# Routing logits from the residual stream, the norm beside them, and the first expert's rows by one-hot products

## The chip, the cores and the metric

One Trainium2 chip, one of its cores. The engines are TensorE (PE, with its weight loads PEld), VectorE (DVE), ScalarE (ACT), GpSimd (POOL) and SyncE (SP), which here only issues transfers. The metric is the device time of one execution in microseconds (us), the median of several runs.

## The reference

A hybrid decoder layer: an RWKV-7 branch and a block-sparse attention branch are merged and projected, the result is added to the input, and a hierarchical mixture of experts follows. The change lies between the output projection and the first expert. What is computed there, for 512 tokens of width 1024:

```python
x = x + gate1 * jnp.einsum('bsd,de->bse', merged, w_out[l])
h2 = rms_norm(x, ln2_g[l]) * (1.0 + scale2) + shift2
x = x + gate2 * hierarchical_moe(h2, w_rg[l], b_rg[l], w_re[l], b_re[l], w1[l], w3[l], w2[l])

# in hierarchical_moe
p_group = jax.nn.softmax((ht @ w_rg + b_rg).astype(f32), axis=-1)      # 4 groups, the best one is taken
e_logits = (ht @ w_re + b_re).astype(f32).reshape(T, N_GROUPS, EXPERTS_PER_GROUP)
# in the group taken: softmax over 8 experts, the two best, their weights made to sum to pg_top
hid = jax.nn.silu(lax.ragged_dot(xs, w1, sizes)) * lax.ragged_dot(xs, w3, sizes)
ys = lax.ragged_dot(hid, w2, sizes) * weights...                        # 32 experts, width 512
```

## The kernel before

All data is float32. A token tile is 128 tokens, so there are TT = 4 tiles, and KT = 8 blocks of 128 channels. The order of each engine's work is written out by hand; engines wait on semaphores by name and count (`x2_done`, `h2_v`, `out_mm` and so on), and every wait holds up all that stands behind it on its engine.

The output projection is 8 groups of 24 matmuls on PE: four token tiles for the left half of the channels, then four for the right half. `out_mm` counts them. DVE adds each group to the residual stream x (`residual`, two instructions of 512 columns), counted by `x2_done`. ACT squares and sums each half row (`half_square`). When both halves of a tile are there, DVE does `norm2(t)`: sum, the root by ACT, the reciprocal, and for each half h2 = x * r * a2, then h2 + shift2. a2 is the gain (1 + scale2) * ln2_g.

PE then turns h2 (`turn_h2`, 8 transposes for a tile, into banks 2 and 3), ACT copies the turned tile to `h2T` and stores the plain one to the table `h2_table` in memory (`turned_h2`), and PE multiplies `h2T` with the routing weights `w_route` (36 columns: 4 groups and 32 experts) in `logits(t)`, 8 matmuls. Only tile 0 is turned ahead of the last projection group.

DVE adds the bias and picks: group, then expert one and two, each by maximum and comparison. The picks go to PE, which counts each token's rank within its expert (four matmuls). From rank and pick DVE makes `slot_hot`, and PE the slot table (`fill_table`): which token sits in which of the 64 slots of an expert, and with what weight. From it DVE makes `slot_rows`, and POOL gathers 64 rows of `h2_table` for each expert by an indirect DMA (`gather`), two experts ahead. PE turns these rows (`do_rows`), ACT copies them to `xT`, and then `up` (w1 and w3 side by side, 16 instructions each), `turn_hid` and `down` follow for each of 32 experts.

The expert weights are three matrices of 2 MB each, in a ring of three slots (`W1_IN`, `W3_IN`, `W2_IN`). SyncE issues them in the order w1, w3, w2 for each expert. A slot's w1 and w3 are free after `up` of three experts ago (`up_mm`), its w2 after `down` (`w2_mm`). The first loads have other gates, since their slots lie in buffers of the earlier phases: w2 of expert 0 waits for the fourth projection group, everything of expert 1 and w1 of expert 2 for the eighth (`out_mm` 8), w3 of expert 2 (its buffer holds h2) for the stores of h2 and all turns, w2 of expert 2 (its buffer holds `h2T`) for the logits. The tenth load, w1 of expert 3, waits for `up` of expert 0.

## Time and profile before

| | us |
|---|---|
| median of 3 runs | 1155.04 (1154.87 to 1158.41) |
| profiled execution, its own time | 1153.15 |
| its span, first to last instruction | 1151.2 |
| eighth projection group ends | 603.0 |
| picks ready | 622.1 |
| first row gather issued | 630.1 |
| expert 0's up-projection | 641.7 to 651.3 |
| last instruction | 1151.2 |

PE is busy 86% of the span, DVE 40%, ACT 27% and POOL 16%; the mean granted clock of TensorE is 0.943 of its full speed. The page cuts the span into 40 slices of 28.8 us. The busy share of the DMA engines is 9 or more (tenths) in the slices from about 660 us to 1120 us, and the last half of the span is spent on the 32 experts. Times of stretches are read as start and end within the span; "idle before" is the engine's idle time just before an instruction, and the arrow names what ended it.

### The profile page before, as it was taken

Reading aid. Unit: us, or ns where it says so; the run is one execution under the profiler, and the core shown is the slowest. Engines: PE = TensorE matmul, PEld = TensorE weight load, DVE = VectorE, ACT = ScalarE, POOL = GpSimd, SP = SyncE. Lnnn points to the kernel's source line nnn. Section 1 sums busy time; section 2 is a strip of 40 time slices with the busy share of each in tenths; the row PEclk is TensorE's granted clock in tenths of the full one; section 3 lists DMA queues with packets and bytes.
Section 4 is the critical chain, followed back from the end, with each engine's and each line's share of the span. In section 5 each row is a group of like instructions: output and inputs, shape, how many; then the busy total and the mean of one; then the engine's idle time right before and its main releaser. Section 6 shows DMA issues by size and latency. Waiting matters only on the chain.

```text
span 1151.2 us, 18827 instructions
## 1 busy us (share of the span) xinstructions
PE 988.6 (86%) x8256; PEld 646.5 (56%) x8256; DVE 462.4 (40%) x724; ACT 315.7 (27%) x537; POOL 182.5 (16%) x201
## 2 busy tenths in 40 slices
PE   3799999898988889999994799998788787978786
PEld 3567799798985668788784333333333333333332
DVE  4548861635427856676565221111111111111115
ACT  6367752042326861222322111110111011100110
POOL 0000000460994430000000011111011110111101
PEclk9799999898979999999997799999899999999998
DMA  9331121400003047465729699999999999999995
GB/s 365 142 147 55 72 76 38 149 15 3 5 3 147 8 165 256 146 224 179 291 100 389 245 407 408 404 392 405 402 406 409 414 407 401 412 410 416 409 398 204
DMA packets 52578, 285.64 MB, mean 248 GB/s; under 512 B 8970, under 2 KB 13210, under 8 KB 38672
## 3 DMA queue, kind: packets, MB, share of 16 engines
q1 hardware_dynamic: 46432, 272.81, 60.5%
q0 software_dynamic: 5056, 8.31, 2.2%
q10 hardware_dynamic: 1008, 3.31, 0.7%
q8 instruction: 66, 1.08, 0.4%
q14 instruction: 16, 0.13, 0.0%
HBM read 276.19 MB, written 16.25 MB: 254 GB/s over the span
## 4 chain that ended last, share of the span: by engine, by line
PE 58%; DMA 28%; DVE 8%; ACT 3%; issue 2%; SPq 1%; DVEq 0%; ACTq 0%; POOLq 0%
PE banks L1566 26%; DMA w_ring<-in_w 21%; PE banks L2001 11%; PE banks L2015 4%; DMA w_tok<-in_w 4%; DMA zr<-in_w_ada 2%; PE banks L1717 1%; PE banks L1719 1%; PE banks L1732 1%; DMA picked<-h_table,slot_rows 1%; PE banks L1859 1%; DVE tokm_r L1032 1%; DVE ring L1170 1%; PE banks L1607 1%; PE banks L1753 1%
## 5 line engine op out<-in xcount | busy, mean ns | idle before, releaser
L2001 PE MATMUL banks<-w_ring,xT 128*64 128x512 f32 x336 | 151.3, 604 | 30.7 <-DMA w_qkv<-in_w 16.4
L850 ACT ACTIVATE silu_a<-banks 64x512 f32<-64x512 f32 x32 | 18.9, 591 | 408.8 <-PE banks L2002 408.8
L1492 DVE TENSOR_TENSOR hid<-banks,silu_a 64x512 f32<-64x512 f32 x32 | 22.2, 693 | 258.6 <-ACT silu_a L850 258.6
L2001 PEld LDWEIGHTS banks<-w_ring,xT 128*64 128x64 f32 x336 | 45.6, 139 | 128.1 <-issue 128.1
L1480 DVE SCALAR_TENSOR_TENSOR mod<-banks,row_weight,mod 64x512 f32<-64x512 f32 x64 | 47.8, 748 | 164.3 <-PE banks L2015 163.3
L2015 PE MATMUL banks<-w_ring,hidT 128*64 128x512 f32 x352 | 92.1, 671 | 10.4 <-ACT hidT L854 10.4
L2001 PE MATMUL banks<-w_ab,xT 128*64 128x512 f32 x176 | 84.9, 639 | 16.8 <-DMA w_tok<-in_w 16.2
L940 POOL DMA_INDIRECT y_rows<-mod,slot_rows x30 | 27.7, 923 | 402.6 <-DVE mod L1480 387.2
L2002 PE MATMUL banks<-w_tok,xT 128*64 128x512 f32 x176 | 85.1, 640 | 0.0
L2002 PE MATMUL banks<-w_ring,xT 128*64 128x512 f32 x176 | 77.7, 594 | 0.0
L1566 PE MATMUL banks<-x_r,ring_r 128*128 128x512 f32 x192 | 77.1, 401 | 0.6 <-DVE tokm_r L1032 0.6
L2002 PE MATMUL banks<-w_qkv,xT 128*64 128x512 f32 x160 | 73.9, 617 | 0.0
L1566 PE MATMUL banks<-ring_r,hT_r 128*128 128x256 f32 (+1 forms) x224 | 69.3, 332 | 2.0 <-DVE zr_r L1032 2.0
L2001 PEld LDWEIGHTS banks<-w_ab,xT 128*64 128x64 f32 x176 | 25.1, 147 | 71.5 <-issue 70.6
L2015 PEld LDWEIGHTS banks<-w_ring,hidT 128*64 128x64 f32 x352 | 26.0, 153 | 60.1 <-issue 46.7
L1292 DVE SCALAR_TENSOR_TENSOR mod<-ada_buf,small,mod 128x512 f32<-128x512 f32 x64 | 48.0, 750 | 11.1 <-DMA ada_buf<-in_w_ada 6.2
L1994 PEld LDWEIGHTS banks<-consts,picked 64*128 64x128 f32 x256 | 30.6, 200 | 35.8 <-issue 24.3
L1566 PE MATMUL banks<-x_r,tokm_r 128*128 128x512 f32 x128 | 49.8, 389 | 0.0
L701 ACT ACTIVATE ring<-banks 128x512 f32<-128x512 f32 (+1 forms) x64 | 33.1, 517 | 59.4 <-PE banks L1732 27.4
L1566 PE MATMUL banks<-ring_r,x_r 128*128 128x256 f32 x256 | 47.8, 288 | 0.2 <-DVE ring_r L1032 0.2
L1566 PEld LDWEIGHTS banks<-ring_r,hT_r 128*128 128x128 f32 x224 | 42.8, 191 | 6.6 <-issue 2.8
L1994 PE MATMUL banks<-consts,picked 64*128 64x64 f32 x256 | 35.1, 278 | 11.2 <-DMA picked<-h_table,slot_rows 11.2
(367 smaller groups left out, 2182.4 us busy)
## 6 DMA issues: line engine op xcount, KB each, us to landing
w_ring<-in_w SPq DMA_DIRECT2D x54, 2048.0 KB, 36.7
w_tok<-in_w SPq DMA_DIRECT2D x21, 2048.0 KB, 38.9
w_ab<-in_w SPq DMA_DIRECT2D x11, 2048.0 KB, 34.8
w_qkv<-in_w SPq DMA_DIRECT2D x10, 2048.0 KB, 39.4
ada_buf<-in_w_ada SPq DMA_DIRECT2D x64, 256.0 KB, 3.2
tokm<-in_w_gate SPq DMA_DIRECT2D x3, 2048.0 KB, 13.5
ring<-in_w_mix SPq DMA_DIRECT2D x5, 1024.0 KB, 4.8
ring<-in_w_ada SPq DMA_DIRECT2D x2, 2048.0 KB, 14.3
```

The lines of the kernel that those rows point to most:

```text
L701: act.activation(dst.rearrange("p h n -> p (h n)"), src, ACT.Copy).then_inc(solve_a[k], 1)
L850: act.activation(silu_a[:, :], bank[2][0:SLOTS, :], ACT.Silu).then_inc(silu_done, 1)
L940: pool.indirect_dma_start(y_rows, IOA(slot_rows[:, 1, e:e + 1].bitcast(u32), 0), ys[:, e % 2, :], None, bounds_check=2 * SEQ - 1, oob_is_e ...
L1032: dve.tensor_tensor(dst, src, hi_.bitcast(f32), ALU.subtract).then_inc(cut_v, 1)
L1292: dve.scalar_tensor_tensor(mod[:, n, :], ada_buf[:, q % NADA, :], small[:, 8 + k:9 + k], mod[:, n, :], ALU.mult, ALU.add).then_inc(ada_use ...
L1480: dve.scalar_tensor_tensor(dst[:, 512 * n:512 * n + 512], bank[5 + n][SLOTS * n:SLOTS * n + SLOTS, :], weight_of(e), gate2[:, n, :], ALU.m ...
L1492: dve.tensor_tensor(hid[:, :], bank[3][SLOTS:P, :], silu_a[:, :], ALU.mult).then_inc(hid_v, 1)
L1566: mm = pe.matmul(dst, a[i][:, k, col_a], b[l][:, k, col_b], start=(k == 0 and n == 0), stop=(k == nk - 1 and n == 2))
L1994: mm = pe.transpose(turned(b)[:, k, :], picked[0:SLOTS, b, k:D:KT], ident[0:SLOTS, 0:SLOTS])
L2001: pe.matmul(bank[2][0:SLOTS, :], xT[:, b, k, :], w1[:, k, :], start=(k == 0), stop=(k == KT - 1))
L2002: mm = pe.matmul(bank[3][SLOTS:P, :], xT[:, b, k, :], w3[:, k, :], start=(k == 0), stop=(k == KT - 1))
L2015: mm = pe.matmul(bank[5 + n][SLOTS * n:SLOTS * n + SLOTS, :], hidT[:, k, :], w2[:, k, 512 * n:512 * n + 512], start=(k == 0), stop=(k == 3))
```

## The change

- The norm's scale r is one number for a token, so it can be taken out of the product with the routing weights: logits = r * (x @ (gain * w_route)) + (shift2 @ w_route + bias). PE turns x instead of h2 (`turn_x2`, one half tile at a time, in the order `x2_turns`), as soon as `residual` has made it, between the projection groups. The logits of a tile have a bank of their own, and DVE scales them by r and adds the bias (`logits_of`).
- For that the gain and the shift are turned into columns (`norm_columns`, 16 transposes of one row), the routing weights are multiplied by the gain column on DVE, and PE computes shift2 @ w_route (`route_bias`, 8 matmuls).
- `norm2` is now one half tile at a time and stands between the residuals; the half (3, 1) comes after the picks. The stores of h2 are a step of their own on ACT (`store_h2`), the last one behind both exponentials.
- After the logits PE does 20 matmuls of the identity with itself, whose result is not used (`keep_running_to_picks`).
- Expert 0's rows are not gathered. DVE makes `first_hot` (token by slot, for expert 0) from the first column of the ranks, and PE computes the turned rows as h2 times `first_hot` (`first_rows`, 8 blocks of 4 matmuls, 64 columns each), half of them ahead of the slot table and half behind it. POOL gathers from expert 1 on.
- w2 of expert 2 is issued before w3 of expert 2; the latter waits for the stores and for `first_rows`, which read h2 there.
- The sum and reciprocal of the group's exponentials move behind the picks. Several semaphores are merged (`s_late`, `ov_in`).

The core of the diff:

```diff
             def load_w13(e):
...
                 if e == 2:
+                    load_w2(2)
                     sp.wait_ge(h2_stored, 16 * TT)
-                    sp.wait_ge(h2t_mm, KT)
+                    sp.wait_ge(xt_mm, 1)
                 sp.dma_start(W3_IN[c], w3_src[e]).then_inc(w3_in[c], 16)
...
+            turned_x2(0)
+            turned_x2(1)
+            spread(0)
+            turned_x2(2)
+            turned_x2(3)
+            turned_x2(4)
+            spread(1)
+            store_h2(0)
+            turned_x2(5)
+            spread(2)
+            turned_x2(6)
+            spread(3)
+            turned_x2(7)
+            store_h2(1)
+            store_h2(2)
+            for i in range(1, 3):
                 act.wait_ge(exp_in, i)
                 ap = gtmp if i == 1 else stats[5]
                 act.activation(ap, ap, ACT.Exp).then_inc(exp_out, 1)
+            store_h2(3)
...
-            gather(0)
             gather(1)
+            gather(2)
...
+            def logits_of(t):
+                dve.wait_ge(logit_mm, t + 1)
+                return dve.scalar_tensor_tensor(L[:, t, :], bank[LOGIT_BANK[t]][:, 0:NR], ln_stat[:, 12 + t:13 + t], b_route, ALU.mult, ALU.add)
...
+            residual(TT)
+            norm2_scale(0)
+            dve.wait_ge(cols_mm, 1)
+            dve.tensor_copy(rt[:, 1000:1016], bank[1][:, 496:512]).then_inc(cols_v, 1)
+            norm2(0, 0)
+            norm2(0, 1)
+            residual(TT + 1)
+            dve.wait_ge(cols_mm, 2)
+            seq(dve.tensor_tensor(b_route, b_route, bank[1][:, 0:NR], ALU.add))
+            dve.tensor_tensor(w_route, w_route, gain_col.unsqueeze(2).to_broadcast([P, KT, NR]), ALU.mult).then_inc(cols_v, 1)
...
+            residual(TT + 3)
+            norm2_scale(3)
+            for t in range(TT - 1):
+                logits_of(t)
+            norm2(3, 0)
+            seq(logits_of(3))
...
+            norm2(3, 1)
+            ranks_of_first = bank[1][:, 0:TT * NEXP].rearrange("p (t n) -> p t n", n=NEXP)[:, :, 0]
+            dve.wait_ge(rank_mm, 1)
+            seq(dve.tensor_copy(first_rank, ranks_of_first))
+            for t in range(TT):
+                ins = dve.tensor_scalar(first_hot[:, t, :], const("slot_id"), first_rank[:, t:t + 1], PICKS[:, t, 0:1], ALU.is_equal, ALU.mult)
+            ins.then_inc(cols_v, 1)
...
                     mm = three_passes(bank[4 + j % TT][:, :], (m_hi, m_lo), cut_views(i), k,
                                       slice(P * (j % TT), P * (j % TT) + P), slice(0, 512))
+                    if j == 2 * TT - 1 and k == 4:
+                        turn_x2(6)
                 mm.then_inc(out_mm, 1)
-                if j == 2 * TT - 2:
-                    turn_h2(0)
...
+                if j == TT:
+                    turn_x2(0)
+                    turn_x2(1)
+                    norm_columns()
+                elif j == TT + 1:
+                    turn_x2(2)
+                    turn_x2(3)
+                    turn_x2(4)
+                    pe.wait_ge(s_late, 96)
+                    route_bias()
+                elif j == TT + 2:
+                    turn_x2(5)
+                    logits(0)
+
             logits(1)
             logits(2)
-            turn_h2(3)
-            logits(3).then_inc(logit_mm, 1)
+            turn_x2(7)
+            logits(3)
+            keep_running_to_picks(20)
             pe.wait_ge(picks_v, 1)
...
+            def first_rows(ks):
+
+                for k in ks:
+                    for t in range(TT):
+                        mm = pe.matmul(turned(0)[:, k, :], h2[:, t, k:D:KT], first_hot[:, t, :], start=(t == 0), stop=(t == TT - 1))
+                return mm
+
+            pe.wait_ge(h2_v, 2 * TT)
+            pe.wait_ge(cols_v, FIRST_HOT)
+            first_rows(range(0, 4))
             pe.wait_ge(slots_v, 1)
...
-            do_rows(0)
+            first_rows(range(4, KT)).then_inc(xt_mm, 1)
```

How the instructions stand now, at three places.

PE between the seventh and the eighth projection group (the 128x512 rows are the projection; 36 columns are logits). Before:

```order
L1566 MATMUL banks<-ring_r,hT_r 128x512 x2
L1566 MATMUL banks<-ring_r,zr_r 128x512
L1566 MATMUL banks<-ring_r,hT_r 128x512 x2
L1566 MATMUL banks<-ring_r,zr_r 128x512
L1938 MATMUL banks<-consts,w_qkv 128x128 [waits h2_v]
L1938 MATMUL banks<-consts,w_qkv 128x128 x3
L1938 MATMUL banks<-consts,w_qkv 128x128 [waits h2_v]
L1938 MATMUL banks<-consts,w_qkv 128x128 x3
L1566 MATMUL banks<-ring_r,hT_r 128x512 [waits x2_done]
L1566 MATMUL banks<-ring_r,hT_r 128x512
L1566 MATMUL banks<-ring_r,zr_r 128x512
```

Now, at the same place:

```order
L1615 MATMUL banks<-ring_r,zr_r 128x512
L1615 MATMUL banks<-ring_r,hT_r 128x512 x2
L1615 MATMUL banks<-ring_r,zr_r 128x512
L1987 MATMUL banks<-consts,x 128x128 [waits h2t_a,x2_done]
L1987 MATMUL banks<-consts,x 128x128 x3
L2014 MATMUL banks<-consts,w_tok 128x36 [waits cols_v,h2t_a]
L2014 MATMUL banks<-consts,w_tok 128x36 x7
L1615 MATMUL banks<-ring_r,hT_r 128x512 [waits x2_done]
```

One turn of h2 (8 transposes) has become half a turn of x (4 transposes) and the logits of tile 0. Ahead of the fifth, sixth and seventh group stand the other new pieces, and the turn numbered 6 stands within the eighth.

PE from the picks to the first expert. The rows of 32 and 96 columns right behind the wait for `picks_v` are the ranks, 64x96 is the slot table, and `w_ab` holds w1 of expert 0. Before:

```order
L1976 MATMUL banks<-mod,consts 128x32 [waits picks_v]
L1977 MATMUL banks<-mod,consts 128x96
L1978 MATMUL banks<-mod 128x96
L1979 MATMUL banks<-mod 128x32
L1985 MATMUL banks<-consts,mod 64x96 [waits slots_v]
L1985 MATMUL banks<-consts,mod 64x96 x7
L1994 MATMUL banks<-consts,picked 128x64 [waits rows_in0]
L1994 MATMUL banks<-consts,picked 128x64 x7
L2001 MATMUL banks<-w_ab,xT 64x512 [waits w3_in0,w1_in0,xt_a]
L2002 MATMUL banks<-w_tok,xT 64x512
```

Now:

```order
L2014 MATMUL banks<-consts,w_tok 128x36 [waits h2t_a]
L2014 MATMUL banks<-consts,w_tok 128x36 x7
L2007 MATMUL banks<-consts 128x128 x20
L2055 MATMUL banks<-mod,consts 128x32 [waits picks_v]
L2056 MATMUL banks<-mod,consts 128x96
L2057 MATMUL banks<-mod 128x96
L2058 MATMUL banks<-mod 128x32
L2071 MATMUL banks<-consts,w_qkv 128x64 [waits cols_v,h2_v]
L2071 MATMUL banks<-consts,w_qkv 128x64 x15
L2064 MATMUL banks<-consts,mod 64x96 [waits slots_v]
L2064 MATMUL banks<-consts,mod 64x96 x7
L2071 MATMUL banks<-consts,w_qkv 128x64 x16
```

The wait for gathered rows (`rows_in0`) and the 8 transposes are gone; 32 products of h2 (in `w_qkv`) take their place, on both sides of the slot table, with a wait for `first_hot` and the last half of h2.

SyncE from the fourth load of the ring (w1 of expert 1) to the twelfth. Before, the fifth row here (`w_qkv`) is w3 of expert 2 and the sixth (`w_tok`) its w2; now the fifth is w2 and the sixth w3. Before:

```order
L455 DMA w_ring<-in_w 128x4096 [waits out_mm]
L459 DMA w_ring<-in_w 128x4096
L469 DMA w_ring<-in_w 128x4096
L455 DMA w_ring<-in_w 128x4096
L459 DMA w_qkv<-in_w 128x4096 [waits h2t_mm,h2_stored]
L469 DMA w_tok<-in_w 128x4096 [waits logit_mm]
L455 DMA w_ab<-in_w 128x4096 [waits up_mm]
L459 DMA w_tok<-in_w 128x4096
L469 DMA w_ring<-in_w 128x4096 [waits w2_mm]
```

Now:

```order
L461 DMA w_ring<-in_w 128x4096 [waits out_mm]
L466 DMA w_ring<-in_w 128x4096
L476 DMA w_ring<-in_w 128x4096
L461 DMA w_ring<-in_w 128x4096
L476 DMA w_tok<-in_w 128x4096 [waits logit_mm]
L466 DMA w_qkv<-in_w 128x4096 [waits xt_mm,h2_stored]
L461 DMA w_ab<-in_w 128x4096 [waits up_mm]
L466 DMA w_tok<-in_w 128x4096
L476 DMA w_ring<-in_w 128x4096 [waits w2_mm]
```

The last two loads of the first nine have changed places, and w3 of expert 2 waits for the turned rows of expert 0 instead of the last turn of h2.

## Rows read from the trace of the kernel before

**Rows 1.** windows: us, busy (x) of each engine, PEclk, DMA share, GB/s.
```profile
604.00:628.00 24.00, 13.14 (x101) 12.51 (x101) 13.49 (x49) 5.87 (x12) 0.00 (x0) 0.75 1.01 413
628.00:629.00 1.00, 0.68 (x5) 0.38 (x3) 0.25 (x2) 0.00 (x0) 0.00 (x0) 0.50 0.14 49
629.00:642.00 13.00, 1.49 (x10) 1.25 (x12) 7.94 (x41) 0.98 (x2) 2.25 (x3) 0.50 0.97 341
642.00:652.00 10.00, 10.00 (x48) 3.47 (x44) 0.00 (x0) 1.49 (x2) 0.72 (x1) 0.76 0.07 18
652.00:1100.00 448.00, 379.54 (x1751) 152.50 (x1750) 66.30 (x95) 45.45 (x87) 53.70 (x58) 0.95 1.01 406
```

**Rows 2.** chain of waits from 700 us: start us, us, what.
```profile
774.93 41.21 DMA w_tok<-in_w
```

**Rows 3.** timeline, SyncE: start us, us, queue, line, issue, out<-in.
```profile
603.04 0.33 SPq L455 DMA_DIRECT2D w_ring<-in_w  x1
...
604.37 0.51 SPq L455 DMA_DIRECT2D w_ring<-in_w  x1
...
628.52 1.30 SPq L469 DMA_DIRECT2D w_tok<-in_w  x1
651.32 0.33 SPq L455 DMA_DIRECT2D w_ab<-in_w  x1
```

**Rows 4.** chain of waits, 550 to 660 us: start us, us, what.
```profile
630.09 9.69 DMA picked<-h_table,slot_rows
...
641.00 0.61 ACT xT L845
...
641.65 1.12 PE banks L2001
```

**Rows 5.** timeline, PE: start us, us, line, instruction, out<-in, shapes, count [idle before].
```profile
596.48 1.04 PE L1938 MATMUL banks<-consts,w_qkv 128*128 128x128 f32 x8
...
607.32 3.66 PE L1945 MATMUL banks<-consts,w_tok 128*128 128x36 f32 x32
...
612.13 1.97 PE L1945 MATMUL banks<-consts,w_tok 128*128 128x36 f32 x16 [0.25 <-ACT w_tok L821]
622.16 0.64 PE L1976 MATMUL banks<-mod,consts 128*128 128x32 f32 x2 [8.05 <-DVE mod L1395]
...
625.86 2.82 PE L1985 MATMUL banks<-consts,mod 128*64 128x96 f32 x16 [1.78 <-DVE mod L1423]
```

**Rows 6.** timeline, DVE, the same columns.
```profile
607.37 0.74 DVE L1345 SCALAR_TENSOR_TENSOR w_qkv<-x,consts,mod 128x512 f32<-128x512 f32 x1
...
614.22 0.31 DVE L1372 TENSOR_TENSOR consts<-banks,consts 128x144 f32<-128x144 f32 x1 [5.38 <-PE banks L1945]
...
615.60 0.18 DVE L1376 TENSOR_TENSOR consts<-consts 128x16 f32<-128x16 f32 x1
...
616.47 0.17 DVE L1381 TENSOR_SCALAR consts<-consts 128x16 f32<-128x16 f32 x1
...
621.46 0.64 DVE L1395 TENSOR_TENSOR mod<-mod 128x32 f32<-128x32 f32 x3
...
625.11 0.69 DVE L1423 TENSOR_TENSOR mod<-consts 128x512 f32<-128x512 f32 x1
```

**Rows 7.** timeline, PE, 22 to 27 us, while the clock falls.
```profile
22.64 0.36 PE L1546 MATMUL banks<-small,tokm 128*128 128x1 f32 x2
22.87 0.36 PE L1547 MATMUL banks<-small,tokm 128*128 128x1 f32 x2
...
26.20 0.56 PE L1547 MATMUL banks<-small,tokm 128*128 128x1 f32 x2
26.62 0.56 PE L1546 MATMUL banks<-small,tokm 128*128 128x1 f32 x2
```

**Rows 8.** DMA issues of 611 to 613 us: x, KB, us to landing.
```profile
h_table<-w_qkv ACTq DMA_DIRECT2D x1, 512.0 KB, 16.2
```

**Rows 9.** windows, columns as in rows 1: 332 to 343 us.
```profile
332.00:343.00 11.00, 10.26 (x177) 10.10 (x177) 1.53 (x3) 1.28 (x5) 10.39 (x10) 0.53 0.01 1
```

More of the change, by code:

```diff
@@ L475, in _ @@
                 load_w13(e)
-                load_w2(e)
+                if e != 2:
+                    load_w2(e)
             for b in range(2):
@@ L1336, in residual, with norm2_scale @@
                 dve.tensor_tensor(xx, xx, out_sc[:, j % 4, :], ALU.add).then_inc(x2_done, 1)
-            def norm2(t):
+            def norm2_scale(t):
                 dve.wait_ge(ssq2, TT + 2 * t + 1)
@@ new lines, in norm_columns, with route_bias @@
+            def norm_columns():
+                pe.wait_ge(cols_v, GAIN2)
+                for i, row in enumerate((mod[0:1, 4:6, :], mod[0:1, 2:4, :])):
+                    row = row.rearrange("p a n -> p (a n)")
+                    for k in range(KT):
+                        at = 496 + KT * i + k
+                        mm = pe.transpose(bank[1][:, at:at + 1], row[:, P * k:P * k + P], ident[0:1, 0:1])
+                mm.then_inc(cols_mm, 1)
+            def route_bias():
+                pe.wait_ge(cols_v, COLUMNS)
+                for k in range(KT):
+                    mm = pe.matmul(bank[1][:, 0:NR], shift_col[:, k:k + 1].to_broadcast([P, P]), w_route[:, k, :], start=(k == 0), stop=(k == KT - 1))
+                mm.then_inc(cols_mm, 1)
@@ L1941, in logits, with keep_running_to_picks @@
+            def keep_running_to_picks(n):
+                for _ in range(n):
+                    pe.matmul(bank[2][:, 0:P], ident, ident, start=True, stop=True)
             def logits(t):
+                pe.wait_ge(h2t_a, TT + t + 1)
+                if t == 0:
+                    pe.wait_ge(cols_v, ROUTE_W)
                 for k in range(KT):
-                    if k % 4 == 0:
-                        pe.wait_ge(h2t_a, 2 * t + k // 4 + 1)
-                    mm = pe.matmul(bank[0][:, NR * t:NR * t + NR], h2T[:, k, P * t:P * t + P], w_route[:, k, :], start=(k == 0), stop=(k == KT - 1))
@@ L1946, in logits @@
-                return mm
+                    mm = pe.matmul(bank[LOGIT_BANK[t]][:, 0:NR], h2T[:, k, P * t:P * t + P], w_route[:, k, :], start=(k == 0), stop=(k == KT - 1))
+                mm.then_inc(logit_mm, 1)
             for j in range(2 * TT):
```

118 lines of the change are left out of this document (58 added, 60 removed).

## The prediction

> **What bounds the kernel now.** I read the windows first, then SyncE's timeline, the chain of waits, and the timelines of PE and DVE around the norm and the routing. From 652 us on the kernel is a stream of expert weights: the DMA share is 1.01 at 406 GB/s until 1100 us [rows 1], and in the chain a load is on the path with 41.21 us from issue to landing [rows 2]. Every us after 652 is therefore bytes over bandwidth, and the change does not touch those bytes. What can be won lies before. The ring of three slots takes nine loads (experts 0 to 2). Seven of them are issued by 604.37, with a wait on the last out-projection matmul at 603.04; the last two come at 628.15 and 628.52, after the h2 rows are stored and the logits are done; the tenth is issued at 651.32, when expert 0's up-projection has ended [rows 3]. The DMA engines are full from 604 to 628 (413 GB/s), nearly idle for 1 us, busy again from 629 to 642, and then idle for ten: 18 GB/s between 642 and 652 [rows 1]. That hole is what the change aims at. Expert 0 is late because its rows are fetched from memory: the gather takes 9.69 us, the copy of the turned rows ends at 641.6 and the up-projection starts at 641.65 [rows 4].
>
> So the end of the kernel follows the later of two times. One is E, when expert 0's up-projection ends and frees its slot. The other is D, when the first nine loads, the stores and two gathers are through. Before, E = 651.3 and D = 641.5. Nothing flows before 652, so from the issue at 651.32 to the first bytes I count 1.1 us: the stream restarts at 652.4.
>
> **The change, step by step.**
>
> PE before the last out-projection ends. Every out-projection group is 5.44 us. Before, one turn of h2 (8 transposes) stands between groups 7 and 8; it costs 0.88 us of the 1.04 shown, 0.11 each [rows 5]. Now there stand in front of the end of group 8: seven turns of x (28 transposes, 3.1 us); 16 one-column turns of gain and shift; 8 bias matmuls; 8 matmuls of logits(0). The logits of a tile are 16 instructions, two for each matmul; 32 take 3.66 us, so 16 take 1.76 in a row [rows 5], and I give the bias and logits(0) 1.76 each. No row shows a one-column turn of one partition. The nearest are the transposes at 0.11: 1.76 us, with 0.6 as the lower end if a load of one row is cheap. The fifth turn reuses a bank whose copy by ACT takes 0.6 us [rows 4]: 0.5 of stall. Sum: 3.1 - 0.9 + 1.8 + 1.8 + 1.8 + 0.5 = 8.0 us, 6.5 to 9. The eighth group ends at 611.0 instead of 603.0, and so do the four loads that wait for it start 8 us later. This is the price of the change.
>
> D. Before, the same bytes went through in 36.0 us: from 604.3 (1.2 after the issues) to 641.5, less the hole of about 1.2 us. In the new order the w2 load of expert 2 waits only for the logits (issued near 618), and its w3 load waits for the end of the one-hot products (637 or later). The five loads and three stores ahead of it keep the engines busy until 612.3 + 29.2 = 641.5 (12.06 MB at 413 GB/s). So the hole at 628 is gone, unless the products end after 640. D = 612.3 + 36.0 = 648.3, between 646.8 and 649.3.
>
> Logits. logits(1) and (2) end at 614.6. The last turn, its copy and logits(3) follow: 0.44 (four transposes of 0.11), 0.85 (a copy of 0.6 with the hand-overs) and 1.96 [rows 4, 5], thus 617.9, where before it was 614.1. The scaled logits stand at 618.1. DVE's pieces of the norm (0.75 and 0.69 us each, [rows 6]) lie beside these matmuls; only norm2(3, 0) is near, from 615.2 to 616.7, and is hidden.
>
> Picks. Before, 614.56 to 622.1, with an exponential waited for, a sum and a reciprocal in between (615.8 to 616.5) [rows 6]. Without these 0.7 us the chain is 6.9: picks at 625.1, 3.0 later than before.
>
> One-hot rows. DVE does norm2(3, 1) (1.44) while PE ranks the picks (1.9 us, [rows 5]); the copy of the ranks and four 64-column compares at about 0.2 follow: 628.0. The weights and slots then take 3.75 us instead of 3.35: 631.8. PE does 32 matmuls of 64 columns, 64 instructions, half of them before the slot table and half after. Their price hangs on TensorE's clock, and here the trace speaks clearly: with 128 stationary columns and one moving column two instructions start 0.23 us apart at the full level and 0.42 apart after the clock had fallen to 1.2 GHz [rows 7], 0.11 and 0.21 each. So 7.1 us or 13.6 us. Moving 64 columns fits under the weight load at both levels. The slot table costs 1.4 or the 2.8 of the row, which ran at 0.50.
>
> The Trainium skill ("TensorE: Matmul & The Clock Gate", LDWEIGHTS) gives a weight load as its columns over 1.2 GHz, 107 ns whatever the level. By that the products would be an estimated 6.8 us at either level (64 times 107 ns), and the slow rival C below would fall away. The rows speak against it, and they decide.
>
> E. Warm throughout: 628.0 + 3.5, slot table from 631.8 to 633.2, + 3.6 = 636.8; copy 0.65; up-projection 6.85 (it is 9.6 in the trace, with five us at half clock): E = 644.3. With the clock low for the first five us: 646.8. Both are before D less the 1.1 us, 647.2, so in both cases D decides.
>
> Beside this. Store 3 now leaves at 626.9 instead of 611.9. A store took 16.2 us beside full queues [rows 8], but that was the third in a row; behind one that lands at 628 or so, I expect 635. The gathers of experts 1 and 2 then land near 646, and PE meets them at E + 0.9: at most 1 us of stall after E, in a stretch where DMA is ahead. One gather fewer is 0.26 MB in the old hole, worth nothing. The merged semaphores and the overflow loop cost nothing here. The queue behind the waiting w3 load on SyncE holds only loads that wait for E anyway.
>
> **Sum.** The stream restarts at 648.3 instead of 652.4: 4.1 us less. Against its own 1153.15 (span 1151.2) the profiled execution would be 1149.0. That execution lies 1.9 below the median of 1155.04; on the median I get 1150.9, with 1149 to 1152 for this case.
>
> **Rivals.**
>
> A, the forecast: E is early enough and D decides, 1150.9.
>
> B, the clock stays low for part of the products. PE idles from the end of the 20 filler matmuls (40 instructions at 0.11 from 617.9: 622.3) to the picks, and again for some 1.5 us until first_hot. Before, it fell to 0.50 after the logits and was still there at the slot table [rows 1, 5]. If it rises near 640, E is 649 to 651 and the gain is 0 to 2.3: 1154.
>
> C, slower: the clock does not rise before the up-projection. What speaks for it is the stretch from 332 to 343 us, where PE was 93% busy with small matmuls and had 0.53 of its clock [rows 9]. Products and table would be 6.8 + 2.8 + 7.0 from 628.0, 644.6, copy to 645.3, up-projection at the old 9.6: E = 654.9, 3.6 later than 651.3: 1158.6. It turns from gain to loss when products and table together exceed 13 us, with the up-projection then cold as before. Against it: the products keep PE without a gap for over 7 us, and the filler shortens the idle time from 8 us to under 3.
>
> D', the change does not do what it says: out-projections are held up by more than counted (a turn that waits for DVE's residual, since DVE now does the norm between residuals). With 12 us instead of 8 the gain is gone: 1155. Each residual has over 2 us of slack in my timetable, so this is unlikely.
>
> **Chances.** A 0.53, B 0.18, C 0.22, D' 0.07. A measurement of this kernel tells 0.3%, 3.5 us, from no change. A lies just beyond it: of its 0.53 I give 0.40 to faster and 0.13 to the same; B and D' are the same; C splits, 0.17 slower and 0.05 the same; 0.02 of B goes to faster. Faster 0.42, same 0.41, slower 0.17. The range leaves out the tails of A and C: 1148.5 to 1159.0.
>
> **What would show it.** Right: the last out-projection ends near 611; DMA without a hole from 612 to the end; up-projection of expert 0 ends before 647; the tenth load is issued then. B or C: PEclk of 0.5 between 628 and 645 and products at 0.21 us per instruction. Wrong altogether if the stream after the restart has another length than the 470 us of before, or if the out-projection ends elsewhere than 609.5 to 612.

## The result, and the profile after

The changed kernel takes 1160.13 us (median of 20 runs), the kernel before 1154.7 us beside it: a ratio of 1.0042, with an interval of 1.0027 to 1.0057. By the ratio that is 4.8 us slower (by the two medians 5.4) where 4.1 us faster was forecast, and 1.1 us above the top of the range that I gave. The profiled execution has a span of 1157.0 us, where the one before had 1151.2.

The windows after, with the columns of [rows 1] (us, busy time of PE, PEld, DVE, ACT, POOL, then the granted clock of TensorE, DMA share, GB/s):

```profile
612.00:628.00 16.00, 13.24 (x86) 12.70 (x85) 11.09 (x46) 3.24 (x7) 0.00 (x0) 0.79 0.97 404
628.00:642.00 14.00, 13.91 (x62) 13.60 (x63) 6.25 (x23) 0.00 (x0) 1.54 (x2) 0.63 0.92 387
642.00:652.00 10.00, 9.31 (x31) 5.84 (x33) 5.26 (x31) 1.88 (x2) 0.51 (x1) 0.54 0.53 184
652.00:662.00 10.00, 9.52 (x60) 4.63 (x58) 1.30 (x5) 1.46 (x3) 0.00 (x0) 0.94 0.51 180
```

The hole that the change aims at has not gone. It lay at 642 to 652 and now lies at about 641 to 657, and one load fills less than half of it. SyncE's timeline (start, duration, queue, line, issue) shows why, beside [rows 3]:

```profile
580.08 0.33 SPq L476 DMA_DIRECT2D w_ring<-in_w  x1
610.46 0.33 SPq L461 DMA_DIRECT2D w_ring<-in_w  x1
618.33 0.33 SPq L476 DMA_DIRECT2D w_tok<-in_w  x1
646.63 0.33 SPq L466 DMA_DIRECT2D w_qkv<-in_w  x1
657.27 0.33 SPq L461 DMA_DIRECT2D w_ab<-in_w  x1
```

The load at 610.46 waits for the eighth projection group: 7.4 us later than before. The load of w3 of expert 2 waits for the end of the one-hot products and leaves at 646.63. The tenth load waits for expert 0's up-projection and leaves at 657.27 instead of 651.32. PE's timeline says where that time is (beside [rows 5]):

```profile
618.11 6.75 PE L2007 MATMUL banks<-consts 128*128 128x128 f32 x40
628.09 7.90 PE L2071 MATMUL banks<-consts,w_qkv 128*128 128x64 f32 x32 [1.57 <-DVE consts L1447]
635.92 2.82 PE L2064 MATMUL banks<-consts,mod 128*64 128x96 f32 x16
638.67 7.88 PE L2071 MATMUL banks<-consts,w_qkv 128*128 128x64 f32 x32
647.24 1.11 PE L2090 MATMUL banks<-w_ab,xT 128*64 128x512 f32 x1 [0.69 <-ACT xT L870]
```

The one-hot products (L2071) take 7.9 us for each half, 15.7 us in all, with the slot table's 2.75 between them. The up-projection starts at 647.24 at half clock and ends at 657.2.

### The profile page after: what moved, and what is told of

It reads as the page before. It is cut to its first block, busy times and chain, and to the rows that moved or that the text cites. A ratio compares the mean times of both kernels' runs of the same rounds, so it can differ in the third digit from the quotient of the medians.

```text
span 1157.0 us, 19096 instructions
## 1 busy us (share of the span) xinstructions
PE 1017.1 (88%) x8384; PEld 672.5 (58%) x8384; DVE 464.8 (40%) x735; ACT 316.0 (27%) x537; POOL 181.6 (16%) x200
## 4 chain that ended last, share of the span: by engine, by line
PE 59%; DMA 27%; DVE 8%; ACT 3%; issue 2%; SPq 1%; DVEq 0%; ACTq 0%
PE banks L1615 26%; DMA w_ring<-in_w 21%; PE banks L2090 11%; PE banks L2104 4%; DMA w_tok<-in_w 4%; DMA zr<-in_w_ada 2%; PE banks L1766 2%; PE banks L2071 1%; PE banks L1768 1%; PE banks L1781 1%; PE banks L1908 1%; PE banks L2014 1%; DVE tokm_r L1057 1%; DVE ring L1195 1%; PE banks L1656 1%
## 5 line engine op out<-in xcount | busy, mean ns | idle before, releaser
L2104 PE MATMUL banks<-w_ring,hidT 128*64 128x512 f32 x352 | 93.6, 680 | 10.4 <-ACT hidT L879 10.4
L1615 PEld LDWEIGHTS banks<-x_r,ring_r 128*128 128x128 f32 x192 | 37.5, 195 | 9.1 <-DVE tokm_r L1057 1.0
## 6 DMA issues: line engine op xcount, KB each, us to landing
w_ring<-in_w SPq DMA_DIRECT2D x54, 2048.0 KB, 36.2
```

Of the source, the lines that this page charges most:

```text
L1615: mm = pe.matmul(dst, a[i][:, k, col_a], b[l][:, k, col_b], start=(k == 0 and n == 0), stop=(k == nk - 1 and n == 2))
L2104: mm = pe.matmul(bank[5 + n][SLOTS * n:SLOTS * n + SLOTS, :], hidT[:, k, :], w2[:, k, 512 * n:512 * n + 512], start=(k == 0), stop=(k == 3))
```

## A ruler for the runs

Profiled executions differ by up to 8 us before anything of interest here starts: the fourth projection group ends between 578.9 and 586.4. So I read each trace from that point, which SyncE marks by its load of w2 of expert 0 (580.08 in the rows above). Three stretches remain: from there to the end of the eighth group (called g8 from here on, read at the first load that waits for it), from g8 to the issue of the tenth load (E, the end of expert 0's up-projection), and from E to the end of the span. The "sum against before" adds the three for one trace and subtracts the 570.9 of before; the ratio is that of the timed runs, each beside runs of the kernel before. D is the prediction's other time, when the first nine loads are through.

| kernel | to g8 | g8 to E | E to end | sum against before | ratio, interval |
|---|---|---|---|---|---|
| before | 22.7 | 48.3 | 499.9 | | |
| after | 30.4 | 46.8 | 499.7 | +6.1 | 1.0042, 1.0027–1.0057 |
| 1 routing from x alone | 30.4 | 48.1 | 499.1 | +6.8 | 1.0066, 1.0039–1.0093 |
| 2 one-hot rows alone | 22.7 | 54.9 | 498.6 | +5.3 | 1.0033, 1.0011–1.0055 |
| 3 roles swapped | 30.4 | 31.5 | 504.8 | -4.1 | 0.9965, 0.9946–0.9984 |
| 4 before, roles swapped | 22.7 | 38.4 | 498.8 | -11.0 | 0.9919, 0.9890–0.9948 |
| 5 contiguous loads | 30.4 | 37.5 | 500.0 | -3.1 | 0.9994, 0.9971–1.0017 |
| 6 no filler | 30.4 | 47.1 | 499.7 | +6.4 | 1.0068, 1.0049–1.0088 |
| 7 filler up to the products | 30.4 | 45.1 | 498.9 | +3.6 | 1.0067, 1.0043–1.0092 |
| 8 pieces behind the projection | 26.7 | 37.1 | 499.7 | -7.4 | 0.9926, 0.9903–0.9948 |
| 9 as 4, clock kept before the picks | 22.7 | 38.1 | 500.6 | -9.5 | 0.9899, 0.9877–0.9920 |
| 10 as 3, delayed | 30.4 | 36.1 | 499.8 | -4.6 | 0.9960, 0.9942–0.9977 |
| 11 as 4, delayed | 22.7 | 43.1 | 499.1 | -6.0 | 0.9937, 0.9918–0.9956 |
| 12 as 9, no gap before the products | 22.7 | 35.7 | 502.1 | -10.4 | 0.9888, 0.9861–0.9916 |

The last stretch is 498.6 to 500.6 us in twelve of the fourteen, whatever was changed in front of it. The two others, 3 and 12, are those with the shortest way from g8 to E: there something else than E decides. The sum of one trace and the ratio of several runs (4 to 20 of each kernel) agree within about 3 us; an interval is 3 to 7 us wide. Only run 7 lies 4 us apart.

## The experiments

**Runs 1 and 2: the two halves of the change apart.** Run 1 keeps the routing from x and gathers expert 0's rows again.

```diff
+            gather(0)
             gather(1)
-            gather(2)
...
-            first_rows(range(0, 4))
...
-            first_rows(range(4, KT)).then_inc(xt_mm, 1)
+            do_rows(0)
```

> The changed kernel with expert 0's rows gathered from memory again, as before the change; everything else of the change stays. It prices the routing from x (with the norm beside it) alone. My theory now: the later start of everything (eighth projection group near 610.5, picks near 625) and the late store of the last half tile (landing near 637.8 in the trace of the change) hold the gather to about 638; expert 0's up-projection then ends near 656 against 651.3 before, so the time is 4 to 5 us over that of the kernel before. Rival (the loss is all in the one-hot products): the up-projection ends by 653 and the time is within 1.5 us of before.

E came 48.1 us after g8, as in the kernel before (48.3), and g8 itself 7.7 later: 0.66% slower, 7.6 us, more than the 4 to 5 expected. The gather was as late as expected (27.9 us after g8, 638 against 610.5 in the expectation), but from the gather to E the trace has 20.2 us and the expectation had only 18. SyncE, then the last store of h2 from ACT's timeline and the gather from POOL's:

```profile
614.03 0.33 SPq L461 DMA_DIRECT2D w_ring<-in_w  x1
...
662.17 0.33 SPq L461 DMA_DIRECT2D w_ab<-in_w  x1
```

```profile
630.38 0.33 ACTq L839 DMA_DIRECT2D h_table<-w_qkv  x1
...
641.94 1.10 POOL L959 DMA_INDIRECT picked<-h_table,slot_rows  x1 [61.83 <-DMA h_table<-w_qkv]
```

The gather waited for the last store of h2 (the releaser behind the arrow), which now leaves behind the picks and lands 11 us after it was issued. The slot numbers that the gather needs were ready at 637.4, some 4 us earlier. Counted from g8 the gather comes after 27.9 us, where it was 27.1. So the routing from x alone is a loss: it puts 7.7 us in front of g8, and the 4 us that the picks gain behind g8 are eaten by the late store.

Run 2 is the kernel before with the one-hot rows of the change.

```diff
+            pe.wait_ge(hot0_v, 1)
+            first_rows(range(0, 4))
             pe.wait_ge(slots_v, 1)
...
-            do_rows(0)
+            first_rows(range(4, KT)).then_inc(xt_mm, 1)
```

> The kernel before with only the one-hot rows of the change (the same 32 products, the same split around the slot table, w2 of expert 2 issued ahead of its w3); h2 is turned and multiplied as before. Theory that a product instruction costs 0.245 us whatever the clock: hot columns ready near 625.4, 7.9 us, table 2.8, 7.9 us, copy 0.7, up-projection 9.6: it ends near 654.3, 3.0 after that of the kernel before, and the time is 3 us longer. Rival (the price hangs on the clock, 0.11 or 0.21): 652 at the latest, no loss; with 0.11 a gain of 5 us.

0.33% slower, 3.8 us, against the 3 of the theory; its rival (no loss) is out. In its profiled execution the clock had fallen at 610, ahead of the last logits, and the ranks start 23.0 us after g8 where they started 19.1: 3.8 us of its E (54.9 after g8) are no part of the edit. The remaining 51.1 are the 654.3 of the expectation. The products took 7.91 and 7.89 us again; over the first half (630 to 638) the granted clock was 0.50 all the way:

```profile
630.42 7.91 PE L2002 MATMUL banks<-consts,w_qkv 128*128 128x64 f32 x32 [1.36 <-DVE consts L1409]
638.26 2.75 PE L1995 MATMUL banks<-consts,mod 128*64 128x96 f32 x16
640.94 7.89 PE L2002 MATMUL banks<-consts,w_qkv 128*128 128x64 f32 x32
```

Each half of the change is a loss by itself, 7.6 and 3.8 us, but the two do not add up: together they lose 4.8. With the one-hot rows no gather of expert 0 waits for the late store any more. What the routing from x still costs in the changed kernel shows at the first product: 48.0 us after the fourth group, against 45.1 in run 2 (48.9 less the 3.8 of its early clock).

**Run 5: what a product costs.** One index is changed: 128 neighbouring columns of h2 are loaded as weights and not every eighth. (The channels of expert 0's rows are then in the wrong order, so this kernel serves only for its time.)

```diff
-                        mm = pe.matmul(turned(0)[:, k, :], h2[:, t, k:D:KT], first_hot[:, t, :], ...)
+                        mm = pe.matmul(turned(0)[:, k, :], h2[:, t, P * k:P * k + P], first_hot[:, t, :], ...)
```

> The changed kernel whose 32 products load 128 neighbouring columns of h2 in place of every eighth one; the count, the shapes and the moved columns stay, and expert 0's turned rows come out in another channel order, so its part of the output is not the layer's. Theory (the stride in the loaded weights is the price): an instruction takes 0.11 us at 2.4 GHz and 0.21 at 1.2, so the products take 7 to 13.5 us in place of 15.7 and expert 0's up-projection ends 2 to 9 us nearer to the eighth projection group than the 46.8 of the changed kernel. Rival (128 rows of weights with 64 moved columns cost 0.245 in any layout, or another user of the memory port holds them up): 0.245 again and no gain.

The weight loads of this line in the changed kernel, and then in run 5 (duration ns min/median/max, first and last start):

```profile
L2071 PEld LDWEIGHTS banks<-consts,w_qkv x64: 312/336/338, 628.1 to 646.0; 128*128 128x128 f32 x64
```

```profile
L2071 PEld LDWEIGHTS banks<-consts,w_qkv x64: 186/192/333, 627.4 to 639.3; 128*128 128x128 f32 x64
```

With the stride, every load takes 312 to 338 ns. Without it, 192 at the full clock and 333 at 1.2 GHz. The halves of the products in run 5, the first mostly at 1.2 GHz and the second mostly at 2.4:

```profile
627.47 5.74 PE L2071 MATMUL banks<-consts,w_qkv 128*128 128x64 f32 x32 [1.56 <-DVE consts L1447]
...
635.85 3.79 PE L2071 MATMUL banks<-consts,w_qkv 128*128 128x64 f32 x32
```

15.7 us became 9.4, the up-projection found a full clock (6.9 us instead of 9.8), and E came 9.4 us earlier in the trace. By the ratios, 0.9994 against 1.0042, 5.5 us were won; the two intervals do not touch. The theory held. The clock's part in the price is seen in the changed kernel itself, in finer windows:

```profile
633.00:634.00 1.00, 1.00 (x6) 1.00 (x5) 0.00 (x0) 0.00 (x0) 0.00 (x0) 0.50 0.96 410
...
641.00:642.00 1.00, 1.00 (x6) 1.00 (x6) 0.90 (x4) 0.00 (x0) 0.69 (x2) 1.00 0.13 25
...
645.00:646.00 1.00, 1.00 (x6) 1.00 (x5) 1.00 (x11) 0.00 (x0) 0.00 (x0) 0.50 0.00 0
```

PE has the same six product instructions in a us (those that reach over its edges counted) at 1.00 and at 0.50, with DMA full and with DMA idle. From 628.09 to 635.92, where the table starts, are 32 instructions, 0.245 us each. So neither the clock nor the transfers set this price.

The Trainium skill has a sentence for it ("SBUF — State Buffer", Door 1: The DMA port swizzle, in its note on cachelines): consecutive reads of one 16-byte line run at full bandwidth, each crossing to a new line pays, and four float32 values is how far one can stride for free. Every eighth float32 puts each value into a line of its own. The trace agrees in that the load with the stride is longer, 336 ns against 192 at the full clock. The page gives no price for it and says nothing of the clock; that this is the mechanism, no run here shows by itself.

**Runs 6 and 7: the filler and the clock.** Run 6 leaves the 20 unused matmuls out, run 7 adds 8 more behind the ranks, so that PE has no gap before the products.

```diff
-            keep_running_to_picks(20)
```

> The changed kernel without the 20 unused matmuls between the logits and the picks. If a product costs 0.245 at either clock: the ranks take 1.9 us in place of 1.1 and nothing else moves; under 1 us longer than the changed kernel. Rival (the clock sets the price of products): the clock is at 1.2 GHz from the logits to the up-projection and the time is 3 us or more longer.

```diff
+            keep_running_to_picks(8)
             pe.wait_ge(h2_v, 2 * TT)
             pe.wait_ge(cols_v, FIRST_HOT)
             first_rows(range(0, 4))
```

> The changed kernel with 8 more unused matmuls between the ranks and the first product (1.8 us, in PE's idle time of 1.6), so that PE has no gap before the products. Theory: the products still take 0.245 us each, the clock still falls to 1.2 GHz among them, and the time is that of the changed kernel within 1 us. Rival (the short gap is what loses the clock): the clock stays at 2.4 GHz through the table and the up-projection, which then takes 6.9 us in place of 9.8: 3 to 4 us less.

Run 6: ranks 1.9 us in place of 1.1, E 0.3 us later in the trace, the products 7.91 and 7.88. The ratio is 1.0068 against 1.0042 and the intervals overlap: 3 us by the ratios, under 1 by the trace, so the time decides nothing between the expectation and its rival. The products at 7.9 us with the filler left out speak for the expectation. Run 7, its first half of the products and the windows behind:

```profile
628.66 7.79 PE L2071 MATMUL banks<-consts,w_qkv 128*128 128x64 f32 x32
```

```profile
628.00:633.00 5.00, 5.00 (x27) 5.00 (x25) 3.77 (x13) 0.00 (x0) 0.00 (x0) 1.00 1.00 420
...
634.00:640.00 6.00, 6.00 (x31) 5.66 (x30) 0.68 (x4) 0.00 (x0) 0.00 (x0) 0.50 1.01 426
640.00:644.00 4.00, 4.00 (x19) 4.00 (x18) 3.54 (x15) 0.00 (x0) 2.05 (x2) 0.93 0.49 178
644.00:648.00 4.00, 3.31 (x15) 3.13 (x16) 3.83 (x24) 0.92 (x2) 0.00 (x0) 0.50 0.07 25
```

More than half of these 32 instructions ran at the full clock, and they took 7.79 us all the same. Then the clock fell though PE was busy without a gap, came back and fell again. So the clock is lost without the gap of 1.6 us before the products too, some 4 us later than in the changed kernel, and keeping it up ahead of them does not shorten them. The trace has E 1.7 us earlier than the changed kernel; 1.5 of these lie in the up-projection, where the full level came back sooner (8.3 us in place of 9.8). The ratio says the opposite, 1.0067 against 1.0042, with overlapping intervals and only four timed runs: whether the kernel got faster or slower is left open.

**Runs 3 and 4: the same rows with the operands changed over.** The one-hot columns become the loaded weights, contiguous and 64 wide; h2 is moved, 512 columns at a time, both halves side by side. The 64 rows come out unturned, ACT copies them to where a gather would put them, and the turn of every other expert follows.

```diff
+            def first_rows():
+                for t in range(TT):
+                    pe.matmul(bank[5][0:SLOTS, :], first_hot[:, t, :], h2[:, t, 0:512], start=(t == 0), stop=(t == TT - 1))
+                    mm = pe.matmul(bank[6][SLOTS:P, :], first_hot[:, t, :], h2[:, t, 512:1024], start=(t == 0), stop=(t == TT - 1))
+                mm.then_inc(cols_mm, 1)
...
-            first_rows(range(4, KT)).then_inc(xt_mm, 1)
+            pe.wait_ge(cols_v, FIRST_HOT + 2)
+            turn_rows(0).then_inc(xt_mm, 1)
```

> The changed kernel with the operands of the one-hot products changed over: the 64 one-hot columns are loaded as weights and h2 is moved, 512 columns at a time, left and right half side by side (16 instructions, 8 pairs); ACT copies the 64 rows to the place of the gathered ones, and they are turned as a gathered expert's are. Theory (the weight loads of h2 are the price): the products take 3.4 to 6.8 us in place of 15.8, copies and turn 3, so expert 0's up-projection ends between 642 and 648 and the first nine loads (648) decide: 3 to 4 us less than before. Rival (the clock or a wait elsewhere is the price): it ends after 651 and nothing is won over the kernel before.

PE's timeline of run 3, first and last pair of products, slot table, turn, up-projection:

```profile
629.95 0.61 PE L2072 MATMUL banks<-w_qkv,consts 128*64 128x512 f32 x1 [1.56 <-DVE consts L1450]
...
632.98 0.59 PE L2072 MATMUL banks<-w_qkv,consts 128*64 128x512 f32 x1
633.01 0.59 PE L2073 MATMUL banks<-w_qkv,consts 128*64 128x512 f32 x1
...
633.53 1.53 PE L2067 MATMUL banks<-consts,mod 128*64 128x96 f32 x16
635.00 1.09 PE L2085 MATMUL banks<-consts,picked 64*128 64x64 f32 x8
636.78 0.64 PE L2092 MATMUL banks<-w_ab,xT 128*64 128x512 f32 x1 [0.69 <-ACT xT L870]
```

The products take 3.6 us in place of 15.7, from hot columns that are ready as late as in the changed kernel. To this comes the turn of the rows, 1.1 us; ACT's two copies lie beside the slot table. The clock stays up over all of it (630 to 640 us: granted clock, share and rate stand at the end):

```profile
630.00:640.00 10.00, 9.31 (x56) 4.69 (x58) 7.58 (x29) 3.06 (x4) 0.00 (x0) 1.00 0.99 419
```

The gap of 1.56 us ahead of the products is that of the changed kernel, to 0.01 us. The clock falls there a us after the gap and stays here: what differs is the form of the products. E comes 31.5 us after g8, and the stream restarts not at E but when the first loads have drained: 504.8 is 5.2 more than the usual 499.6, so the stream goes as if the tenth load had been issued 36.7 us after g8. The time is 0.35% under before, 4.0 us. This is the gain that the prediction forecast, reached by another form of the products.

Run 4 puts this form into the kernel before, without the routing from x.

```diff
+            pe.wait_ge(hot0_v, 1)
+            first_rows()
             pe.wait_ge(slots_v, 1)
...
-            do_rows(0)
+            pe.wait_ge(hot0_v, 3)
+            turn_rows(0).then_inc(xt_mm, 1)
```

> The kernel before with the one-hot rows in the form of the swapped roles, no turning of x: the eighth projection group ends at 603 as before, products from 625.4, rows turned by 636, up-projection of expert 0 ends between 643.5 and 646.5 and the first nine loads near 641.5. Theory that the end follows the later of the two: 5 to 7.5 us less than before. Rival (the length of the stream after the restart isn't fixed, what is won is given back later): under 2 us.

```profile
606.50 0.33 SPq L458 DMA_DIRECT2D w_ring<-in_w  x1
...
634.76 0.33 SPq L464 DMA_DIRECT2D w_qkv<-in_w  x1
644.94 0.33 SPq L458 DMA_DIRECT2D w_ab<-in_w  x1
```

E is 38.4 us after g8 where it was 48.3, g8 is not delayed, and the time is 0.81% less: 9 us, more than the 5 to 7.5 expected, since E came some 2 us ahead of its range (38.4 us after g8, where 643.5 less 603 is 40.5). The windows show that a short hole is left, and that half of the products ran at 1.2 GHz:

```profile
625.00:632.00 7.00, 5.01 (x16) 2.92 (x18) 4.75 (x18) 0.20 (x1) 0.00 (x0) 0.50 1.03 436
...
643.00:646.00 3.00, 3.00 (x28) 1.79 (x25) 2.17 (x14) 0.59 (x1) 0.00 (x0) 1.00 0.31 63
```

**Runs 10 and 11: is the end really the later of two times?** The same 20 unused matmuls, 4.7 us, in front of the turn of expert 0's rows, once where E has slack (run 3) and once where it has none (run 4).

```diff
+            keep_running_to_picks(20)
             pe.wait_ge(cols_v, FIRST_HOT + 2)
             turn_rows(0).then_inc(xt_mm, 1)
```

> The changed kernel with swapped roles, and 20 unused matmuls (4.4 us at 2.4 GHz) in front of the turn of expert 0's rows. There expert 0's up-projection ended at 643.9, and by the length of the stream behind it (499 us from the tenth load to the end) the restart counted as one at 649.3: 5 us of slack. Theory that the end follows the later of the two: the time of the swapped roles within 1 us (1150.8, 0.35% under before). Rival (every us of expert 0 counts): 4.4 us more.

> The same 20 unused matmuls in the kernel before with swapped roles, where the transfers had a hole of 3 us before the tenth load. Theory: 4.4 us more than without them, so 4.5 to 5 us under before (ratio near 0.996). Rival (stream and stores decide there too): no change, ratio 0.992.

In run 10, E moved from 31.5 to 36.1 us after g8 and the stretch behind it shrank from 504.8 to 499.8: the delay vanished, 0.9960 against 0.9965. In run 11, E moved from 38.4 to 43.1, the stretch behind it stayed (498.8, 499.1), and the ratio went from 0.9919 to 0.9937. In the traces E moves by 4.6 us both times, and only in run 11 does the end move with it. The ratios of run 11 and run 4 differ by 2.1 us and their intervals overlap; by the ratio alone the rival (no change, 0.992) is not excluded, so this branch rests on the trace.

**Run 8: fewer pieces ahead of the eighth group.** On the kernel of run 3:

```diff
-                    if j == 2 * TT - 1 and k == 4:
-                        turn_x2(6)
...
-                elif j == TT + 2:
-                    turn_x2(5)
-                    logits(0)
...
+            turn_x2(4)
+            turn_x2(5)
+            logits(0)
+            turn_x2(6)
             logits(1)
+            turn_x2(7)
             logits(2)
```

> The kernel of the swapped roles with the turns 4 to 6 and the logits of tile 0 moved behind the eighth projection group, and the norm of the last tile ahead of the scaled logits on DVE. If the first nine loads decide there (they start with the eighth group), that group ends 3.4 us earlier and so does everything: 3 to 3.5 us less than with the swapped roles alone, 7 less than the kernel before. Rival (the logits come later by what the loads win, and expert 0 decides): no change against the swapped roles alone.

g8 came 26.7 us after the fourth group in place of 30.4, and the ratio fell from 0.9965 to 0.9926. That is 4.5 us less than run 3, where 3 to 3.5 were expected. But during the logits, now in one row behind the projection, the clock fell:

```profile
617.00:631.00 14.00, 14.00 (x69) 14.00 (x69) 6.50 (x26) 2.36 (x4) 0.00 (x0) 0.51 1.01 425
```

PE was busy for all of the 14 us and had half its clock. E was 37.1 after g8, with a small hole in the transfers, so both times decide nearly together. Even so this version only draws level with run 4, which has no routing from x at all.

**Runs 9 and 12: the clock in the best version.** Run 9 is run 4 with 24 unused matmuls between logits and picks; run 12 has 33 there and 7 more behind the ranks. The diff is that of run 12.

```diff
             logits(3).then_inc(logit_mm, 1)
+            for _ in range(33):
+                pe.matmul(bank[2][:, 0:P], ident, ident, start=True, stop=True)
...
+            for _ in range(7):
+                pe.matmul(bank[2][:, 0:P], ident, ident, start=True, stop=True)
             pe.wait_ge(hot0_v, 1)
```

> The kernel before with the one-hot rows in swapped roles, and 24 unused matmuls between the logits and the picks. With the swapped roles alone, the clock was at 1.2 GHz until 632.7 (ranks 1.9 us, half of the products at half speed) and the transfers had a hole of 3 us before the tenth load. Theory: the clock is at 2.4 GHz from the picks on, expert 0's up-projection ends 2.5 to 3 us earlier, the hole closes, and the time is 2 to 3 us less than with the swapped roles alone, 11 less than before. Rival (the first nine loads decide by then): under 1 us.

> The kernel before with the one-hot rows in swapped roles, 33 unused matmuls between the logits and the picks and 7 between the ranks and the products, so that PE has nearly no gap from the logits to the products (with 24 and none there was a gap of 2.6 us, and the clock fell to 1.2 GHz within the ranks). Theory (a gap loses the clock there): it stays at 2.4 GHz, the products take 3.5 us in place of 5.6, the up-projection of expert 0 ends 36 us after the eighth projection group in place of 38.1, the hole in the transfers closes and the time is 1.5 us less than with 24. Rival (the clock falls among small matmuls without a gap too): products 5.6 us as before and no change.

Run 9: the clock was full to the picks, fell within the ranks, and the products took 5.7 us as in run 4; E moved by 0.4 us. That expectation failed. The window from the picks on:

```profile
624.00:630.00 6.00, 4.59 (x16) 2.49 (x18) 4.23 (x15) 0.20 (x1) 0.00 (x0) 0.54 1.01 427
```

PE had stood idle for 2.6 us before the ranks and for 1.4 before the products. Run 12 shortened the first gap to 0.6 and closed the second, and the clock stayed up throughout:

```profile
616.00:627.00 11.00, 10.18 (x89) 9.75 (x87) 6.71 (x33) 2.58 (x4) 0.00 (x0) 1.00 1.01 427
627.00:630.00 3.00, 2.97 (x24) 2.73 (x26) 1.76 (x10) 0.21 (x1) 0.00 (x0) 1.00 1.05 444
630.00:643.00 13.00, 12.26 (x72) 5.49 (x69) 10.15 (x46) 3.06 (x4) 2.05 (x2) 1.00 1.01 416
```

The products took 3.5 us and E came 35.7 after g8. Against before, run 12 is 1.1% faster (1142.93 against 1155.21 us). The 1.5 us expected over run 9 are not shown: the intervals of runs 4, 9 and 12 overlap, and the trace of run 12 gains little, since the stretch behind E is 502.1. E is early there and no longer decides, as in run 3.

## Why the prediction was wrong

Point by point, by its own steps.

**What bounds the kernel: right.** The end follows the later of E and D. From the tenth load to the end it is 499.9 us before and 499.7 after (the 470 us that the prediction names among its signs is not what the trace of before has there), and runs 3, 10 and 11 show both branches.

**PE ahead of the eighth group: right.** 8.0 us forecast, 7.7 measured (30.4 against 22.7). Two misses in opposite directions hide in that. The 16 one-column turns took 1.1 us (1.76 forecast), the bias 1.7 (1.76):

```profile
586.31 1.16 PE L1996 MATMUL banks<-consts,mod 1*128 1x1 f32 x16
...
594.80 1.87 PE L2002 MATMUL banks<-consts 128*128 128x36 f32 x16
```

The stall for ACT's copy was some 0.5 us, as forecast. What the sum left out is that the four projection groups themselves take 0.5 us more with the new pieces between them: 22.3 in place of 4 times 5.44.

**Logits, picks, hot columns: right in the numbers, in part by luck.** Forecast 617.9, 625.1 and 628.0; in the trace the logits end at 618.1, the ranks start at 625.44 and the first product at 628.09. But the clock fell during the logits of the last tile, which took 3.0 us and not 1.96, and the turn ahead of them came 0.8 us earlier than forecast. The filler, too, ran at half clock to 622 and ended at 624.9 and not at 622.3:

```profile
615.08 3.22 PE L2014 MATMUL banks<-consts,w_tok 128*128 128x36 f32 x16 [0.69 <-ACT w_tok L831]
```

**The one-hot products: wrong, and this is the step that failed.** Forecast 7.1 us at the full clock or 13.6 at half; measured 15.7. The price was taken from [rows 7], matmuls whose weights are whole neighbouring columns. The products load every eighth column. The trace of before had a row of that very kind, the turn of gathered rows, which the prediction did not look up. Its loads (ns min/median/max):

```profile
L1994 PEld LDWEIGHTS banks<-consts,picked x256: 182/202/208, 639.8 to 1114.3; 64*128 64x128 f32 x128
```

They are longer than the loads of h2's turns, which take neighbouring columns (143 ns in the mean, at the full clock), with half the partitions. And the slowest of the 256 is 208: those of expert 0, which ran at 0.50 of the clock, cost no more than the rest. A load that is dearer with the stride, and whose price does not move with the clock, was to be seen there; the size at 128 partitions was not. And [rows 5] had said that the slot table takes 2.8 us at half clock; that end, not the 1.4, came true.

The prediction set aside a rule of the Trainium skill ("TensorE: Matmul & The Clock Gate", LDWEIGHTS: columns over 1.2 GHz, with no term for the level) because of the rows. For whole-row loads that was right again: 0.118 and 0.21 us an instruction in run 5. For the loads at hand the time was indeed the same at both levels, but at 0.245 and not 0.107 us, so the rule would have missed by more.

**The clock: wrong, the second step that failed.** I took it as kept by long, gapless work and gave rival C 0.22. PE was busy from 628.1 to 646.6 without a gap and had the full clock for only some 5 us of it (the clock fell in the window from 629, and again in that from 643), and the up-projection started at half clock as before:

```profile
629.00:630.00 1.00, 1.00 (x5) 1.00 (x6) 0.96 (x3) 0.00 (x0) 0.00 (x0) 0.61 1.03 434
...
643.00:644.00 1.00, 1.00 (x6) 1.00 (x6) 0.83 (x5) 0.00 (x0) 0.00 (x0) 0.50 0.55 160
```

C said 1158.6 and E = 654.9; E was 657.3. What C lacked is again the price of the strided load, 15.7 against 13.8 us. Together the miss of E is 13.0 us over the 644.3 forecast: 8.6 from the products, 1.4 from the table, 3.0 from the up-projection. The first is the stride's price, the other two are the clock's. The clock falls without the stride too: in run 5, with neighbouring columns and everything else alike, it was at 0.50 from 629 to 633. Why it falls among products of this form and not among the swapped ones, no run here settles.

**D: right in principle, and hidden.** Forecast was a tenth load as if issued at 647.2 with g8 at 611.0, so 36.2 after it; run 3 has 36.7. In the changed kernel E lies 10 us behind that. There D itself was late too, since w3 of expert 2 waits for the products; I had set 640 as the point from which this matters, and the products ended at 646.6. The last store landed at 637.8 where I expected 635; behind the long products that cost nothing, in run 1 it held up the gather.

**The sum.** With D deciding, 4.1 us were to be won; run 3, which has the same front and short products, won 4.0. With products, table and up-projection at what they measured, the same sum gives E = 628.0 + 7.9 + 2.8 + 7.9 + 0.7 + 9.8 = 657.1, and so 5.8 us more than before: the profiled execution took 5.8 more, and by the ratio it is 4.8.

## What to carry to other kernels

Before a matmul's price is taken from a row, compare how its weights lie in memory and not only the shape: here a stride of eight float32 made each load 75% longer at the full clock (336 ns against 192) and as slow as a load without the stride is at half clock (333). When one operand of a product is needed with a stride, see if it can be the moved one or if the narrow operand can be loaded: 16 instructions with 64 loaded columns took 3.6 us, and the turn that they need behind them 1.1, where 64 instructions with 128 strided columns took 15.7. And count a piece that is moved ahead of the event that starts the transfers at its full price there, before counting what it saves later: the routing from x cost 7.7 us ahead of g8, against 4 gained behind it.

## What the runs showed of the hardware

- A weight load of 128 columns, every eighth float32, on 128 partitions: 336 ns at the full clock and at 1.2 GHz. The same columns without stride: 192 and 333 ns. On 64 partitions, every eighth float32, turning gathered rows: 200 ns at 1.2 GHz (expert 0 in the trace of before) and 203 at the full clock (the experts behind it). Neighbouring columns on 128 partitions, turning h2: 140 ns at the full clock (before) and 230 at 1.2 GHz (run 2). So the kind of instruction matters too, and what part of the step from 200 to 336 is due to the partitions wasn't tried.
- A PE that is busy all the time does not keep its clock. It fell to 1.2 GHz within the strided products: in the changed kernel a us behind a gap of 1.6 and again at 643 with no gap for 15 us, in run 7 at about 633.5 with no gap for 7 us. It fell within the same products without the stride as well (run 5, 0.50 from 629 to 633). In run 8 it was at 1.2 GHz for 14 us of logits and filler. In runs 3 and 12 it was at 2.4 GHz through the swapped products, and in run 4 it rose among them.
- One execution's front part differs by up to 8 us from another's, and the stretch behind the tenth load only by 2 where expert 0 decides. The stretch from the fourth group to g8 repeats within 0.1 us among kernels with the same front (22.7 in six traces, 30.4 in seven), so read from an event near the edit a single trace shows what two medians don't.
